# Two-layer diffusion trunk on one core: eight of layer 0's twelve conditioning blocks moved into the recurrent stage, and eight of the first expert's twelve weight units loaded from the experts' stage

## The reference, cut to what matters

```python
def adaln(cond, w, b):
    m = jax.nn.silu(cond) @ w + b
    return [t[:, None, :] for t in jnp.split(m, ADA_CHUNKS, axis=-1)]   # ADA_CHUNKS = 6

def trunk_layer(x, cond, p, mixer, ctx, rope):
    sh1, sc1, g1, sh2, sc2, g2 = adaln(cond, p['ada_w'], p['ada_b'])
    mix, state = mixer(modulate(rms_norm(x, p['norm1']), sh1, sc1), p, ctx, rope)
    x = x + g1 * mix
    x = x + g2 * ec_moe(modulate(rms_norm(x, p['norm2']), sh2, sc2), p)
    return x, state

# in hybrid_mixer (layer 0), the recurrent branch:
    xc = centred_dwconv(xb, p['conv_w'], p['conv_b'])
    hf = rglru_scan(xc, p['fwd'], h0f, reverse=False)
    hb = rglru_scan(xc, p['bwd'], h0b, reverse=True)
    rec = (hf + hb).astype(h.dtype) * jax.nn.gelu(gb)
    state = (k, v, hf[:, -1].astype(h.dtype), hb[:, 0].astype(h.dtype))

# in ec_moe, for each of 16 experts e:
    hid = jax.nn.silu(jnp.einsum('ecd,edf->ecf', xe, p['w_gate'])) * jnp.einsum('ecd,edf->ecf', xe, p['w_up'])
    ye = jnp.einsum('ecf,efd->ecd', hid, p['w_down']) * gate[..., None].astype(h.dtype)
```

## Time and profile before

| | |
|---|---|
| Median of 3 runs | 3567.45 us (3565.46 to 3567.59) |
| Profiled execution: its time / its span | 3564.61 / 3562.8 us |
| PE, DVE, ACT busy, share of the span | 91%, 63%, 52% |
| HBM read / written | 525.05 / 38.94 MB |
| `modulation` stage | 27.95 to 91.8 us |
| recurrent stage | 103.5 to 294.7 us |
| `routing` of layer 0 | 842.9 to 918.4 us |

### The profile page before, as it was taken

How to read it: one execution, slowest core, us unless ns; L and a number is a source line. 1 busy time by engine, 2 the same in 40 slices (tenths; PEclk the granted TensorE clock), 3 DMA queues, 4 the chain that set the end, 5 groups by cost and what they waited for, 6 DMA issues and landing times. The chain is left out here.

```text
span 3562.8 us, 54970 instructions
## 1 busy us (share of the span) xinstructions
PE 3224.6 (91%) x19994; PEld 2440.3 (68%) x19994; DVE 2250.7 (63%) x2852; ACT 1853.8 (52%) x2550; POOL 559.0 (16%) x319
## 2 busy tenths in 40 slices
PE   6995988897799999998798998989997899999997
PEld 2545777784567667766687887878885576676675
DVE  1457666645466666665676685767755576666665
ACT  2353755621466656564456373554732566665663
POOL 0001000000222232231100101011000233222220
PEclk7998999997899999999899999999997899999999
DMA  9200000136888888884310100100034688888883
GB/s 339 65 18 21 1 3 19 42 112 232 317 294 294 286 295 298 291 289 149 112 39 8 35 6 7 39 7 21 1 125 191 238 289 288 293 294 287 292 301 120
DMA packets 218311, 566.34 MB, mean 159 GB/s; under 512 B 37845, under 2 KB 75418, under 8 KB 217882
## 3 DMA queue, kind: packets, MB, share of 16 engines
q1 hardware_dynamic: 207760, 530.26, 41.2%
q0 software_dynamic: 9472, 33.57, 4.0%
q10 hardware_dynamic: 906, 0.23, 0.0%
HBM read 525.05 MB, written 38.94 MB: 158 GB/s over the span
## 5 line engine op out<-in xcount | busy, mean ns | idle before, releaser
L2318 DVE TENSOR_TENSOR moe_lo<-moe_raw,moeg_hi 128x2048 fp32r<-128x2048 f32 x384 | 883.8, 2336 | 318.8 <-PE psum L2138 154.9
L2220 ACT CAST moeg_hi<-moe_raw 128x2048 fp32r<-128x2048 f32 x384 | 728.8, 1910 | 432.5 <-PE psum L2156 294.9
L913 PE MATMUL psum<-attn_w_hi,attn_hs 128*128 128x256 f32 (+2 forms) x1440 | 382.8, 351 | 82.6 <-DVE attn_w_lo L1261 55.9
L1377 DVE TENSOR_REDUCE attn_neg_max<-psum 128x1 f32<-128x1280 f32 (+1 forms) x216 | 292.4, 1355 | 80.1 <-PE psum L1018 77.8
L913 PEld LDWEIGHTS psum<-attn_w_hi,attn_hs 128*128 128x128 f32 x1440 | 261.2, 195 | 115.3 <-DVE attn_hs L1255 69.8
L1177 ACT ACTIVATE attn_e<-psum,attn_neg_max 128x1280 f32<-128x1280 f32 (+1 forms) x216 | 265.0, 1227 | 79.7 <-DVE attn_neg_max L1377 61.4
L1018 PE MATMUL psum<-attn_ks,attn_qst 128*128 128x512 f32 (+2 forms) x1200 | 283.6, 370 | 16.2 <-ACT attn_qst L1115 6.5
L1115 ACT COPY attn_pt<-psum 128x512 f32<-128x512 f32 (+2 forms) x400 | 192.5, 507 | 153.1 <-PE psum L1031 139.4
L2156 PE MATMUL psum<-moeg_hi,moeh_x_hi 128*128 128x512 f32 x960 | 265.0, 398 | 4.8 <-issue 4.8
L2156 PE MATMUL psum<-moe_lo,moeh_x_hi 128*128 128x512 f32 x960 | 261.9, 394 | 0.0
L2156 PE MATMUL psum<-moeg_hi,moeh_x_lo 128*128 128x512 f32 x960 | 260.3, 392 | 0.0
(11 more groups left out here) (288 smaller groups left out, 5302.5 us busy)
## 6 DMA issues: line engine op xcount, KB each, us to landing
moe_raw<-in_l_w_gate SPq DMA_DIRECT2D x256, 512.0 KB, 3.7
moe_raw<-in_l_w_up SPq DMA_DIRECT2D x256, 512.0 KB, 5.0
moe_raw<-in_l_w_down SPq DMA_DIRECT2D x128, 1024.0 KB, 6.2
ada_w<-in_l_ada_w SPq DMA_DIRECT2D x48, 1024.0 KB, 14.3
out_w<-in_l_w_out SPq DMA_DIRECT2D x16, 512.0 KB, 5.3
h_rows<-mix_xs SPq DMA_DIRECT2D x16, 512.0 KB, 2.6
attnw_w<-in_l_w_in SPq DMA_DIRECT2D x16, 512.0 KB, 6.7
attnw_w<-in_l_w_in SPq DMA_DIRECT2D x6, 1024.0 KB, 8.5
```

The costliest lines, as they stand in the source:

```text
L913: last = pe.matmul(out, hs[t % 2][:, part, k, :], right, start=(k == 0 and n == 0), stop=(k == KB - 1 and n == 2))
L1377: dve.tensor_reduce(neg_max[:, n:n + 1], m.psum[:, score_at(n):score_at(n) + hi - lo], AX.X, ALU.max, negate=True).then_inc(s["maxed"], 1)
L2220: act.copy(mm.hi[slot % 4][:, :, :], mm.raw[slot][:, :, :]).then_inc(s["hi_ready"], 1)
L2318: dve.tensor_tensor(mm.lo[slot][:, :, :], mm.raw[slot][:, :, :], mm.hi[slot % 4][:, :, :].bitcast(F32), ALU.subtract).then_inc(s["lo_ready ...
```

## The change

- Layer 0's conditioning makes blocks 0 to 3 in its own stage (8 halves, all of them already issued in `setup`). Blocks 4 to 11 are made in the recurrent stage, with 4 slots of their own and the row buffers in memory that attention's output takes later.
- There, SP issues 4 halves ahead of attention's loads, two more behind each of the first three chunks' gate loads, and the last six behind the loop, ahead of the store of the states. PE makes one block behind the tasks of each of the chunks 0 to 2, and the other five behind those of chunk 3. ACT copies a block's result between its exponentials in chunks 0 to 2, and the other five behind its last square root. DVE adds the bias behind its loop.
- `adaln` takes a bank for each block: bank 6 for the first four of the eight, then 0, 1, 3 and 4, with a wait for the tasks' last read; bank 7 has the sums.
- SP's, PE's and ACT's loop over chunks is written out in Python; DVE's stays a hardware loop.
- In layer 0's `routing` SP issues only units 0 to 3 of the first expert. Units 4 to 7 and the four of down are issued as the first thing of the experts' stage, with no wait.
- Layer 1 computes and loads as before.

```diff
@@ -231,8 +231,8 @@
 
-    def loads(sp):
-        for x in range(n_slots, halves):
+    def loads(sp, lo=0, hi=halves):
+        for x in range(max(lo, n_slots), hi):
             sp.wait_ge(used, x - n_slots + 1)
@@ -248,13 +248,13 @@
 
-        if i >= 2:
-            pe.wait_ge(row_read, i - 1)
+        if banks[i] in banks[:i]:
+            pe.wait_ge(row_read, max(x for x in range(i) if banks[x] == banks[i]) + 1)
         for half in range(2):
...
             for k in range(4):
-                last = pe.matmul(m.psum[32 * k:32 * k + 32, banks[i % 2] * BANK:(banks[i % 2] + 1) * BANK],
+                last = pe.matmul(m.psum[32 * k:32 * k + 32, banks[i] * BANK:(banks[i] + 1) * BANK],
                                  m.cond[:, 4 * half + k, :], slots[x % n_slots][:, k, :],
@@ -267,7 +267,7 @@
             act.wait_ge(turned, i - 1)
-        act.copy(rows[i % 2][:, :], m.psum[:, banks[i % 2] * BANK:(banks[i % 2] + 1) * BANK]).then_inc(row_read, 1)
+        act.copy(rows[i % 2][:, :], m.psum[:, banks[i] * BANK:(banks[i] + 1) * BANK]).then_inc(row_read, 1)
 
@@ -527,7 +527,7 @@
 
-def recurrent_branch(nc, m, a, sem, h, cat, pre, attn_ahead):
+def recurrent_branch(nc, m, a, sem, h, cat, pre, attn_ahead, ada_at):
 
@@ -536,6 +536,10 @@
     last_h = put("last_h", [P, 2, LC])
+    slots = [put(f"ada{i}", [P, KB // 2, BANK]) for i in range(4)]
+    rows = [m.tensor(f"lru_row{i}", [P, BANK], F32, ada_at + i * BANK * 4) for i in range(2)]
+    ada = adaln(m, a, sem, 0, slots, rows, (6, 6, 6, 6, 0, 1, 3, 4), 7 * BANK, 4, 8)
+    IN_LOOP = LC - 1
     L0, C0 = 1, LAT + 4
@@ -557,8 +561,9 @@
             gates(0)
+            ada.ahead(sp)
             attn_ahead(sp)
-            with sp.Fori(0, LC - 1) as c:
+            for c in range(LC - 1):
 
@@ -566,6 +571,8 @@
                 gates(c + 1)
+                ada.loads(sp, 4 + 2 * c, 6 + 2 * c)
+            ada.loads(sp, 4 + 2 * IN_LOOP)
             sp.wait_ge(s["last_ready"], LC)
@@ -579,7 +586,7 @@
         def _(pe):
-            with pe.Fori(0, LC) as c:
+            for c in range(LC):
                 for n in range(TASKS):
@@ -603,11 +610,19 @@
                     last.then_inc(s["task_done"], 1)
+                if c < IN_LOOP:
+                    ada.product(pe, c)
+                else:
+
+                    for i in range(IN_LOOP, ada.count):
+                        if i == IN_LOOP + 1:
+                            pe.wait_ge(s["task_read"], LC * TASKS)
+                        ada.product(pe, i)
 
...
             act.wait_ge(s["pad_zeroed"], 1)
-            with act.Fori(0, LC) as c:
+            for c in range(LC):
                 act.wait_ge(s["task_done"], c * TASKS + 1)
@@ -632,6 +647,8 @@
                 act.drain()
+                if c < IN_LOOP:
+                    ada.copy(act, c)
                 for d in range(2):
@@ -640,6 +657,8 @@
                     act.activation(bv[d][:, :], rt[d][:, :], ACT.Sqrt).then_inc(s["root_ready"], 1)
+            for i in range(IN_LOOP, ada.count):
+                ada.copy(act, i)
 
@@ -685,6 +704,7 @@
                 dve.drain()
+            ada.vectors(dve)
 
@@ -1846,13 +1866,12 @@
             ada.loads(sp)
-            for k in range(KB):
-                if k >= 4 and l == 0:
-                    ada.wait_free(sp, k - 4)
+            for k in range(4 if l == 0 else KB):
                 mm.load_gu(sp, k, 0)
-            for i in range(4):
-                ada.wait_free(sp, 4 + i if l == 0 else i)
-                mm.load_dn(sp, i, 0)
+            if l == 1:
+                for i in range(4):
+                    ada.wait_free(sp, i)
+                    mm.load_dn(sp, i, 0)
 
@@ -2017,6 +2036,11 @@
 
+            if l == 0:
+                for k in range(4, KB):
+                    mm.load_gu(sp, k, 0)
+                for i in range(4):
+                    mm.load_dn(sp, i, 0)
             for k in range(KB):
@@ -2456,7 +2480,7 @@
         rows = [put(f"row{i}", [P, BANK]) for i in range(2)]
-        ada = adaln(m, a, keep_sem, 0, slots, rows, (0, 1), 2 * BANK, 0, 12)
+        ada = adaln(m, a, keep_sem, 0, slots, rows, (0, 1) * 2, 2 * BANK, 0, 4)
         setup(*shared, ada.ahead)
@@ -2477,7 +2501,7 @@
             if l == 0:
-                recurrent_branch(*shared, h, cat, recurrent_pre, attn_pre[0].ahead)
+                recurrent_branch(*shared, h, cat, recurrent_pre, attn_pre[0].ahead, m.region_at[1])
                 end()
@@ -2487,7 +2511,7 @@
             rows = [put(f"row{i}", [P, BANK]) for i in range(2)]
-            ada = adaln(m, a, sem, 1, slots, rows, (6, 7), 5 * BANK, (0, 10)[l], (10, 2)[l])
+            ada = adaln(m, a, sem, 1, slots, rows, (6, 7) * 5, 5 * BANK, (0, 10)[l], (10, 2)[l])
             routing(*shared, l, mm, drams[l], ada)
```

## The result

Changed kernel 3528.05 us (median of 4 runs, 3525.07 to 3530.04), kernel before 3566.45 us in the same comparison (4 runs, 3560.14 to 3567.59). The ratio is 0.9892, 95% interval 0.9879 to 0.9904: faster by 38.4 us where I had given 48.4. The time is inside the range of 3509 to 3532, but outside the forecast's own of 3515 to 3524; the sum of the terms is 10 us too good.

A forecast was written before the change was run, and what follows sets the result against it. Bounds: loads in conditioning, PE in the recurrent stage (its end the state stores' landing), SP's unit issue at routing's end. -44.2 + 3.3 + 3.0 - 10.5 = -48.4 us from 3567.45 gives 3519.0; range 3509 to 3532.

The forecast's parts named there:

- term 1: Conditioning stage: the 16 halves of blocks 4 to 11 go, so the next stage starts earlier, -44.2 us.
- term 2: Recurrent loop: blocks 4, 5, 6 add PE time in chunks 0 to 2, written-out loops counted as nothing, +3.3 us.
- term 4: Routing's end: stage ends with DVE instead of SP's unit issue, experts starts earlier, -10.5 us.
- term 3: Recurrent stage's tail: slow PE, late last half, or state store queued behind halves 14 and 15, +3.0 us (0 to +3.6).
- A: Rival, long tail: lower clock and late last half, +8 instead of +3, 1 us per chunk's copy; 3527, chance 0.12.
- B: Rival: late unit loads starve the first experts, returning up to routing's whole 10.5 us; 3529.5, chance 0.12.
- at least +2.6: Recurrent tail: smallest cost if queue order keeps the state store's long completion from overlapping halves 14 and 15.
- Cases (a) to (c): Experts' head: ctx_gu's first and second half and expert 1's first units come in time; the last just, or +1.9 us.
- Rival C: Clock stays up: experts' head -1.8, tail at +0, a little in attention's head, -5 us in all; 3514, chance 0.11.
- term 4's better end: Experts' head: if the clock stays up, L2125 takes 3.64 rather than 5.77 us, -1.8; bound -12.3.
- D: Rival: loads only exposed elsewhere, halves 10 to 15 arriving one by one in the tail, +19; 3535, chance 0.05.
- E: Rival, slower: conditioning halves fill the queue, PE waits for w_x and w_g of three chunks; 3590, chance 0.03.

The follow-up runs named there:

- e1: Changed kernel plus one small Tanh behind the square roots of chunks 0 to 2, so the table loads in ACT's idle time; 3524.51 us, one run.
- e2: Kernel before with only the chunk loops on SP, PE and ACT written out; 3580.85 us, one run.
- e3: Changed kernel with both state stores issued from ACT's DMA queue instead of SP's, ahead of its copy of block i=6; 3528.59 us, one run.
- e4: Changed kernel with room for six conditioning halves instead of four in the recurrent stage; 3532.31 us, one run.
- e6: e4 with the second state store issued from ACT's queue instead of SP's; 3529.59 us, one run.
- e7: e4 with each partition's four numbers written side by side, so a state store is 128 pieces of 16 bytes; 3520.33 us, one run.
- e10: e9 with the copies of blocks i=3 and 4 ahead of ACT's last Tanh and square roots; 3513.17 us, median of five.
- e12: e10 with the two state stores not issued until the end of attention's list on SP; 3508.15 us, median of five, ratio 0.9835.
- e5: Kernel before with the routing part of the change alone; 3561.09 us, one run, against 3570.93 for the kernel before beside it.
- e11: Kernel before with PE's and ACT's chunk loops written out and SP's loop kept; 3576.99 us, one run.
- e8: Changed kernel, waiting for the state stores at the end of attention's stage, states and semaphore kept across stages; 3516.43 us, one run.
- e9: Changed kernel with the changes of e1, e4 and e8 together; 3513.18 us, median of five.

## Why the prediction was right, and where it was 10 us off

The mechanisms of term 1, of the blocks in term 2 and of term 4 held. Two things did not: the nothing counted for the written-out loops, and term 3's reason for the late store. The time lies inside the range only because that had been widened for rivals A and B, whose mechanisms did not occur; that much is luck.

**Term 1, conditioning stage, -44.2.** Measured -44.1 (91.86 to 47.77). The step "Behind the last half the same work follows" held to 0.3 us (6.47 for 6.77); the half came 0.4 us later (41.30 for 40.89).

**Term 2, three blocks in the loop, +3.3.** The blocks are as priced: +0.35 in chunk 0, and +1.29, +1.28 in e1 where the table load is out of the way; 2.9 in all. What failed is the sentence "Written-out loops ... I count nothing for them": +1.33 us in each of chunks 1 and 2 (e2), 1.4 by e1, some 4 us with the last chunk, of which 2.7 fall into this term. I had looked for the price in branches, and it was in what the compiler placed. The Trainium skill, "ScalarE activation tables: per-element evaluation and per-set limits", section on table sets in the compiler and the runtime, has the rule: the compiler places the loads per block, each for the longest run that one set serves. If a loop's body is such a block, which the page does not say, the rows agree with it: in the loop the load stood at the body's first ACT instruction (154.68 at L613); written out, the copies and the Square of the next chunk go on with the set of the Sqrts, and the load falls ahead of the first Tanh (134.46 at L640).

**Term 3, the tail, +3.0.** Measured +6.1 (from the last chunk's first row to attention 75.43 us against 69.37). 1.3 of the excess is the table load again. The slow PE was foreseen, and DVE follows 0.5 behind; that 239.29 to 259.97 is 20.7 us where the sum has 20.2 is in part luck. The sum has every block at the lower clock and no wait. In fact the clock was up from 249.5 to 253 us, which saved some 1.8 us, and the last half, put at 6 us from issue to landing, took 9.7 and was awaited 2.58. I had taken +3.0 where the slow PE alone gives +3.6, which is 0.6 more. The last 1.1 us are the store, which lands at 261.5 and not, as in my sum, before PE's end. Here the reason was wrong as well as the size: "it is now queued behind halves 14 and 15". Another queue doesn't help (e3), idle DMA engines don't (e4: 17.5 us), two queues don't (e6); its small pieces set the landing (e7: 2.4 us). What another transfer suffers from them is the other half of the same finding: the half awaited 4.54 us in e3, attention's cache awaited 7.1 us in e10. The Trainium skill, "DMA: Bandwidth & Descriptors", section on queues, rings and completion order, says that a semaphore's increment lands only behind every earlier write of its DMA engine, across queues; e3, e10 and e12 agree with that. It would not give the 17.5 us of e4, where no other transfer is on the way. Nor does the prediction's "at least +2.6" follow from it: by the rule the store lands no earlier than halves 14 and 15, put at about 288 there, which leaves its 293.8 as it was.

**Term 4, routing, -10.5.** Measured -10.1 in the changed kernel and -10.2 alone (e5); the eleven kernels with this part take 62.3 to 65.6 us there, the three without it 75.0 to 75.4. Cases (a) to (c) held: no wait for a raw unit. "All behind experts of layer 0 shifts unchanged" did not: the head gives back 1.7 us (2.8 alone) at the lower clock. Rival C and term 4's better end had the clock right in part and the wait behind it wrong. PE is at the lower clock when experts starts, in all three. The upper clock came back inside 924 to 926 us before (5.5 to 7.5 us behind experts' first row), inside 881.0 to 881.5 after (5.3 to 5.8) and inside 911.5 to 912.0 in e5 (3.1 to 3.6), and the first context product was shorter, 5.77, 5.41 and 4.31 us. But this gains nothing: PE's next work, the first `lat_gu` matmuls, waits for DVE's `moe_lo` and starts 10.9 us behind the first row in all three, so that PE stands for 3.27, 3.63 and 4.72 us. PE's row before:

```profile
929.38 1.16 PE L2156 MATMUL psum<-moeg_hi,moeh_hid_hi 128*128 128x512 f32 x4 [3.27 <-DVE moe_lo L2318]
```

Before, the clock stayed up over that pause; after, it fell at 888.0, 1.4 us into the new work, and in e5 inside 918.0 to 918.5, during the pause. That is the 1.7 and the 2.8 us. `moe_lo` starts when the product is done (926.26, 883.12, 914.70) and takes 2.97, 3.33 and 4.42 us, where the later ones take 2.2; in all three it ends 2.1 us behind the end of GpSimd's subtraction of `moeh_hid_lo` (L2037 before). That the two don't run side by side would fit, but was not tested.

**The base of the sum.** From routing 1 to the last stage the kernel before took 817.8 us in its profile, and all thirteen later profiles took 819.2 to 820.1, e2 and e11 among them, which differ from it in layer 0's recurrent stage alone. So some 2 of the 11 us by which the spans miss look like luck of the one execution that the sum was made against; there is no second profile of the kernel before to tell. The medians of several runs (38.4) don't rest on it, and differ from the spans (37.4) by 1.

**The miss** in the spans is 11.0 us: table loads 2.4 + 1.3, the tail's PE 0.6, its store 1.1, routing 0.4, experts' head 1.7, the base 2.0, 0.2 in terms 1 and 3, and 1.3 scattered over the long stages. The medians have 1.0 less.

**The rivals.** A's 3527 and B's 3529.5 lie nearest to the time, but not by their mechanisms: no copy cost a chunk 1 us and the last half was awaited 2.58 us (A), and no unit was awaited (B). C gave nothing back (term 4). D and E did not happen: w_x of chunk 1 was issued at 88.01, 11.7 us later in the stage than before, which is the 11 foreseen, and no row of L608 or of the w_g products waits for a load. But E's sum has 24.1 us from issue to use where 12.7 were left; no load of w_x took more than 6.5 to land.

**Still open.** Why the second store takes 9.1 to 9.6 us in two kernels (before, e5) and 16.8 to 17.6 in others (e2, e4, e6, e10, e11) with idle DMA engines. It isn't SP's loop (e11) nor the conditioning (e2). PE's and ACT's loops, kept only in the two with the short landing, were not separated from it. That the two outputs' places in memory differ from kernel to kernel would fit too, but was not tested; and each kernel has one trace. Nor was it tested why the kept states go with a quicker layer 1.

## What to carry to other kernels

When a loop is written out, look at ACT's table loads before and after: they move, and one small activation of the next set in ACT's idle time puts them back. Don't end a stage on a store of single numbers: wait for it a stage later, and issue it where no load that is needed soon runs beside it. A stage's price at the end of a prediction is that of its last wait: name every candidate (PE at the lower clock, DVE, the store) and take the latest one, not their middle. And before a faster clock is counted as a gain, look for what the next instruction waits for.

## What the runs showed of the hardware that I had not expected

A store of 2 KB in 512 pieces of 4 bytes lands after 8 to 13 us, a second one beside it after 9 to 19; as 128 pieces of 16 bytes each they land after 1.5 and 2.4 us. In e4 the last packet of either is in the trace 2.1 us behind the first issue; for the rest of the time it shows none. While such stores are on the way, loads of another tensor issued behind them land late: 12 to 14 us in e10, where DVE waited 7.1 us for one, against 1.8 in e12. The landing of one and the same pair can differ by 8 us between kernels with the same code around it (9.6 before, 17.0 in e11), and it came in two sizes only where no other transfer ran: 9.1 and 9.6, or 16.8 to 17.6.

The length of PE's pause ahead of experts does not tell what the lower clock costs behind it. Behind pauses of 12.1 to 12.4 us nothing was lost in the head (before, e2, e11). Behind 1.5 us it was 1.7 us in e1, e3 and e7 and 2.6 to 2.8 in e5, e8 and e9; behind 2.5 to 2.7 us 1.7 or 1.8 in the changed kernel, e4, e6 and e12. In e10, with 2.54, no group ran at the lower clock, and what was lost there, 1.3 us, goes with a wait of 1.55 us for gathered rows.
